# Plain fp32 products in place of the three-product high/low split, with ten slots for weight slabs

## The reference, cut to what matters

```python
def merge(h, fa, db, nc):
    gates = jax.nn.sigmoid(h @ w_g + b_gate)
    g_a, g_b, g_c = jnp.split(gates, N_BRANCH, axis=-1)
    return (g_a * (fa @ w_a) + g_b * (db @ w_b) + g_c * (nc @ w_c)) @ w_out

def conv_ffn(h, w_up, conv_w, conv_b, w_down):
    u = dwconv3(h @ w_up, conv_w, conv_b)
    a, b = jnp.split(u, 2, axis=-1)
    return (jax.nn.silu(a) * b) @ w_down

def _swiglu(x, w_in, w_out):
    a, b = jnp.split(x @ w_in, 2, axis=-1)
    return (jax.nn.silu(a) * b) @ w_out
```

## Time and profile before

| what | value |
| --- | --- |
| median of 3 runs | 2890.88 us (2889.95 to 2892.99) |
| profiled execution, its own time | 2876.13 us |
| its span on the core | 2874.0 us |
| mean granted TensorE clock | 0.969 of full speed |
| TensorE matmuls (PE) | 2656.9 us busy, 92% of the span, 17744 records |
| TensorE weight loads (PEld) | 2317.1 us, 81% |
| VectorE (DVE) | 1699.3 us, 59%, 2800 instructions |
| ScalarE (ACT) | 1335.0 us, 46%, 2136 instructions |
| GpSimd (POOL) | 184.0 us, 6% |
| read from memory | 378.36 MB, 132 GB/s over the span |

### The profile page before, as it was taken

One profiled execution on the slowest core, in us unless ns is written; L12 is line 12 of the kernel. 1 busy time (PEld: TensorE's weight loads), 2 busy tenths in 40 slices (PEclk: granted clock), 3 DMA queues, 4 the chain that ended last, 5 costly groups with the idle time before them and its releaser, 6 DMA issues.

```text
span 2874.0 us, 42224 instructions
## 1 busy us (share of the span) xinstructions
PE 2656.9 (92%) x17744; PEld 2317.1 (81%) x17744; DVE 1699.3 (59%) x2800; ACT 1335.0 (46%) x2136; POOL 184.0 (6%) x239
## 2 busy tenths in 40 slices
PE   5997899998999999899998998999899999978999
PEld 3875676676777777778788997999799999975999
DVE  5245534435676666454556876666666675746665
ACT  5235533324444443454445554455544553565543
POOL 1000000000000000000000001110010110015110
PEclk8998999998999999899999999999999999988999
DMA  7223432122344444232344654644255455530464
GB/s 233 72 85 123 133 99 70 59 88 74 103 161 146 133 133 145 74 103 96 103 140 133 201 186 141 205 162 147 88 177 191 156 183 191 177 106 1 155 198 147
DMA packets 337388, 382.12 MB, mean 133 GB/s; under 512 B 7408, under 2 KB 301296, under 8 KB 337200
## 3 DMA queue, kind: packets, MB, share of 16 engines
q1 hardware_dynamic: 334656, 370.37, 39.5%
q0 software_dynamic: 2544, 9.06, 1.0%
HBM read 378.36 MB, written 1.05 MB: 132 GB/s over the span
## 4 chain that ended last, share of the span: by engine, by line
PE 75%; DVE 11%; ACT 10%; issue 2%; DMA 1%; POOL 0%; SPq 0%; ACTq 0%; DVEq 0%
PE PS L1182 20%; PE PS L1184 19%; PE PS L1183 19%; ACT WH L1521 3%; DVE WL L1842 3%; PE PS L1315 2%; PE PS L1199 1%; PE PS L1201 1%; PE PS L1200 1%; PE PS L1330 1%; DMA RAWB<-in_w_ada 1%; PE PS L1298 1%; DVE TMP L1909 1%; PE PS L1231 1%; PE PS L1213 1%
## 5 line engine op out<-in xcount | busy, mean ns | idle before, releaser
L1842 DVE TENSOR_TENSOR WL<-RAWB,WH 128x1024 fp32r<-128x1024 f32 (+1 forms) x709 | 848.7, 1207 | 608.2 <-ACT WH L1521 606.0
L1182 PE MATMUL PS<-AH,WH 128*128 128x256 f32 (+1 forms) x3072 | 972.8, 317 | 82.1 <-DVE AL L1914 31.0
L1183 PE MATMUL PS<-AL,WH 128*128 128x256 f32 (+1 forms) x3072 | 952.6, 310 | 0.0
L1184 PE MATMUL PS<-AH,WL 128*128 128x256 f32 (+1 forms) x3072 | 952.2, 310 | 0.0
L1521 ACT ACTIVATE WH<-RAWB 128x1024 fp32r<-128x1024 f32 (+1 forms) x709 | 721.9, 1034 | 255.6 <-PE PS L1184 215.6
L1182 PEld LDWEIGHTS PS<-AH,WH 128*128 128x128 f32 x3072 | 586.3, 191 | 157.5 <-issue 52.3
L1183 PEld LDWEIGHTS PS<-AL,WH 128*128 128x128 f32 x3072 | 587.1, 191 | 31.4 <-issue 0.8
L1184 PEld LDWEIGHTS PS<-AH,WL 128*128 128x128 f32 x3072 | 586.2, 191 | 31.7
L1182 PE MATMUL PS<-BH,WH 128*128 128x256 f32 (+1 forms) x1504 | 470.1, 313 | 8.1 <-DVE BL L2010 3.0
L1183 PE MATMUL PS<-BL,WH 128*128 128x256 f32 (+1 forms) x1504 | 457.9, 304 | 0.0
L1184 PE MATMUL PS<-BH,WL 128*128 128x256 f32 (+1 forms) x1504 | 457.8, 304 | 0.0
(11 more groups left out here) (309 smaller groups left out, 2629.7 us busy)
## 6 DMA issues: line engine op xcount, KB each, us to landing
RAWB<-in_f_in SPq DMA_DIRECT2D x88, 1024.0 KB, 5.1
RAWB<-in_w_in SPq DMA_DIRECT2D x52, 1024.0 KB, 5.1
RAWB<-in_w_ada SPq DMA_DIRECT2D x48, 1024.0 KB, 5.5
RAWB<-in_w_up SPq DMA_DIRECT2D x44, 1024.0 KB, 5.1
RAWB<-in_f_out SPq DMA_DIRECT2D x40, 1024.0 KB, 5.1
RAWB<-in_w_down SPq DMA_DIRECT2D x20, 1024.0 KB, 5.1
RAWB<-in_sb_qkv SPq DMA_DIRECT2D x12, 1024.0 KB, 5.1
RAWB<-in_w_out SPq DMA_DIRECT2D x8, 1024.0 KB, 5.2
```

The lines of the kernel that those rows point to most:

```text
L1182: pe.matmul(out, h, xh[:, 0:T], start=k == 0, stop=False)
L1183: pe.matmul(out, h, xl[:, 0:T], start=False, stop=False)
L1184: i = pe.matmul(out, l, xh[:, 0:T], start=False, stop=k == g.kt - 1)
L1842: dve.tensor_tensor(c.part("WL", p), c.raw(p.slab)[:, k0:k1, c0:c1], c.part("WH", p).bitcast(F32), ALU.subtract).then_inc(up("lo", ("lo", ...
```

## The change

All splitting is taken out. `AH` and `AL` become one fp32 buffer `A`, `BH` and `BL` become `B`; `WH`, `WL`, the pieces and the step `split` are gone, and TensorE reads its weights from the slab in `RAWB`. A tile of depth is one fp32 product. `NR` goes from 3 to 10. A slab's slot comes free when TensorE has used the slab (`used`). The results that were copied to a high part are now written straight to `A` or `B`: the shift after a norm, the product of the two halves in the feed-forward parts (by DVE), `sub_scale`, the outputs of the attentions and of the DFT. `w_out` of the first block reads `Y` directly, the factor 0.5 being put into the modulation (`ada_half`). The eight tiles for `kv_norm` are one DVE instruction each (`kv_mul`). The sigmoid of the gates in the last attention becomes exp, add 1 and reciprocal, and the step `sb_table`, which loads an activation table on ACT, moves from behind the gate's product to the first head norm of the queries.

```diff
-NR = 3
-NW = 4
+NR = 10
 SLAB = 2048
-PIECE = 1024
...
     for s in plan.slabs:
         if s.j >= NR:
-            old = plan.slabs[s.j - NR]
-            on.wait_ge(*(at("lo", old.first + len(old.cuts) - 1) if old.cuts else at("used_raw", old.j)))
+            on.wait_ge(*at("used", s.j - NR))
...
         elif kind == "mm":
...
-            on.wait_ge(*at("lo", s.p.p))
+            on.wait_ge(*at("raw", s.p.j))
             for k in range(g.kt):
-                xh, xl = c.operand(g.src, k)
-                h, l = hi[:, k, s.c:s.c + 128], lo[:, k, s.c:s.c + 128]
                 on.wait_ge(*at(*g.ready(k)))
-                pe.matmul(out, h, xh[:, 0:T], start=k == 0, stop=False)
-                pe.matmul(out, h, xl[:, 0:T], start=False, stop=False)
-                i = pe.matmul(out, l, xh[:, 0:T], start=False, stop=k == g.kt - 1)
+                i = pe.matmul(out, w[:, k, :], c.operand(g.src, k)[:, 0:T], start=k == 0, stop=k == g.kt - 1)
...
         elif kind == "mm_tok":
...
-                pe.matmul(out, h, wh, start=k == 0, stop=False)
-                pe.matmul(out, h, wl, start=False, stop=False)
-                i = pe.matmul(out, l, wh, start=False, stop=k == 7)
+                i = pe.matmul(out, c.m["A"][:, k, tk], c.raw(s.p)[:, k, :], start=k == 0, stop=k == 7)
...
         elif kind == "ada":
...
-            for k in range(4):
-                pe.matmul(out, sc_v[:, 4 * i + k, :], hi[:, k, :], start=i == 0 and k == 0, stop=False)
-                t = pe.matmul(out, sc_v[:, 4 * i + k, :], lo[:, k, :], start=False, stop=i == 1 and k == 3)
+            for k in range(8):
+                t = pe.matmul(out, sc_v[:, k, :], c.raw(s.p)[:, k, :], start=k == 0, stop=k == 7)
...
-        elif kind == "split":
...
-            act.activation(c.part("WH", p), c.raw(p.slab)[:, k0:k1, c0:c1], ACT.Copy).then_inc(up("hi", ("hi", p.p)), 1)
...
-        elif kind == "split":
...
-            dve.tensor_tensor(c.part("WL", p), c.raw(p.slab)[:, k0:k1, c0:c1], c.part("WH", p).bitcast(F32), ALU.subtract).then_inc(
-                up("lo", ("lo", p.p)), 1)
...
         elif kind == "nmul":
...
-            act.activation(AH[:, k, a0:a0 + W], x[:, 0:W], ACT.Copy).then_inc(up("acted", ("xhi", name, k)), 1)
+            for i, seg in enumerate(s.x):
+                cols = slice(i * 256, i * 256 + 256)
+                t = act.activation(A[:, k, cols], x[:, cols], ACT.Identity, bias=c.mod(seg[3][0], seg[3][1], k, seg[2]))
+            t.then_inc(up("acted", ("normed", name, k)), 1)
...
-            act.activation(BI[:, 768:864], c.bank(s.b)[:, 0:96], ACT.Sigmoid).then_inc(up("acted", ("ns_gate",)), 1)
+            act.activation(BI[:, 768:864], c.bank(s.b)[:, 0:96], ACT.Exp, scale=-1.0).then_inc(up("acted", ("ns_gate_exp",)), 1)
```

More of the change, by code:

```diff
@@ L135, with __init__ @@
 class Slab:
[L136 to L143, removed]
+    def __init__(self, j, w, k0, kt, c0, cols):
+        self.j, self.w, self.k0, self.kt, self.c0, self.cols = j, w, k0, kt, c0, cols
 class Plan:
-    def __init__(self, slabs):
-        self.known, self.slabs, self.steps, self.put_off = slabs, [], [], []
+    def __init__(self):
+        self.slabs, self.steps, self.put_off = [], [], []
         self.banks = Ring(self, 8)
@@ L213, in run_units, with slab @@
             yield
-    def slab(self, w, k0, kt, c0, cols, cuts=()):
-        j = len(self.slabs)
-        s = self.known[j] if self.known else Slab(j, w, k0, kt, c0, cols, list(cuts))
+    def slab(self, w, k0, kt, c0, cols):
+        s = Slab(len(self.slabs), w, k0, kt, c0, cols)
         self.slabs.append(s)
         return s
[L223 to L239, removed]
     def gemm(self, name, w, col0, ncols, T, src, ready, ev, kt=8, k0=0, width=256, fine=True, x=None, hook=None):
@@ L318, in ada @@
             for half in range(2):
[L319 to L323, removed]
+                s = self.slab(("w_ada", l), 0, 8, (c + 2 * half) * 128, 256)
+                self.add("ada", (l, c), n=half, b=b, p=s)
                 self.tick()
@@ L637, in kv_split @@
     def kv_split(self, k):
-        m = self.tmps.take()
-        x = ([("kv_norm",)], 256, 256)
-        self.add("nmul", ("kv_norm", "ffn1_norm1"), n=k, t=m, x=x)
-        self.add("nlow", ("kv_norm",), n=k, t=m, x=x[1:])
-        self.tmps.give(m, ("xlo", "kv_norm", k))
+        self.add("kv_mul", n=k)
     def swiglu(self, i, l, norm, nrm, mark):
-        ready = lambda k: ("xlo", norm, k)
+        ready = lambda k: ("normed", norm, k)
         self.mark(mark)
@@ L779, in gate_turn @@
             self.add("ns_gturn", b=b, t=g48)
-            self.banks.give(b, ("ns_gate",))
+            self.banks.give(b, ("ns_gate_exp",))
             self.sqs.give(g48, ("ns_gturn",))
@@ L880, in sum, with split @@
             plan.banks.give(self.b, ("sd", self.name))
-    def split(self, name, T, segs, W, a0=0):
+    def split(self, name, T, segs, W):
         plan = self.plan
@@ L908, in __init__ @@
     def __init__(self, plan, name, gain, first=None):
-        self.plan, self.name, self.gain, self.first, self.n, self.low = plan, name, gain, first, 0, None
+        self.plan, self.name, self.gain, self.first, self.n = plan, name, gain, first, 0
     def add(self, k, after):
```

317 lines of the change are left out of this document (90 added, 227 removed).

## The result

The kernel after takes 3271.58 us (median of 4 runs, 3268.26 to 3273.81) against 2890.41 us for the kernel before beside it (4 runs, 2882.74 to 2892.99). The ratio is 1.1323, with a 95% interval of 1.1299 to 1.1346: slower by 381 us, 88 us less slow than the forecast of 3360. The profiled execution took 3271.48 us, its span is 3269.7 us, and its mean clock is 0.993 (before 0.969).

The account below looks back on a forecast made before the run. TensorE, busy 2656.9 of 2874.0 us, was taken as the bound. The profiled 2876.1 + 599 for products - 129 given back = 3346, times 1.005 = 3363, taken as 3360; stated range 3270 to 3450, the forecast's own 3280 to 3440.

Parts of the forecast that it names:

- The products: On TensorE, one plain fp32 product per depth tile replaces the split products: +599 us, all on the path.
- What was given back: Time returned from TensorE's waits, other standing time, clock and restarts, summed to -129 us.
- `WL`: TensorE's waits for the weights' low parts, 44.1 us, would go, with 10 kept for slow first slabs: -34 us.
- Low parts after norms: TensorE's 66.0 us of waits for activations' low parts; the chain stays, its last copy and subtraction go: -27 us.
- The rest of the standing time: TensorE's remaining 107.0 us of many small waits, such as those in attentions; a third would return: -35 us.
- Clock and restarts: On TensorE, a fifth of the half-rate clock loss returns, -18 us; unhidden weight loads after waits, -15 us.
- The scale of 1.005: The sum on the profiled execution, 3346 us, was multiplied by 1.005 for the median of the runs: 3363 us.
- Costed at nothing: The load queue's new wait for TensorE's use of the slab ten back; ten slots give over 60 us of cover.
- Nothing given back: Rival, 8%: the fp32 tiles keep all the waits and each record costs 4 ns more, giving 3535 us.
- weight loads bare: Rival, 4%: stationary tiles load between records, 93 ns more on each of 10,640 records, near 4360 us.
- faster: Rival, 2%: plain products stream at the split products' rate, 0.231 us in place of 0.432, giving 2066 us.
- All of it is given back: Rival, 8%: as DVE and ACT halve, only the start of the standing time remains, giving 3221 us.

Follow-up runs that it names:

- the last experiment: The kernel after with the gate's sigmoid and the place of `sb_table` as they were before: 3283.35 us, ratio 1.1349.
- the thin experiments: Kernels whose weight split instructions touch one column only; both thinned in the kernel before: 2779.97 us, under plain products from `WH`: 3318.66 us.

## Why the prediction was right and where it was not

**The ladder.** One row is one run; standing time is span less busy TensorE of its profile.

```
run                                       median   step   TensorE stands   clock
before                                    2891.6              217.1        0.969
products plain, all splits there          3370.7  +479        147.3        0.983
 + weight split thin                      3318.7   -52        114.9        0.986
 + low parts of activations thin          3311.2    -7        107.3        0.988
 + high copies and their steps gone       3283.4   -28         92.0        0.992
   (the change with old tables)
 + tables moved: the kernel after         3271.6   -12         83.6        0.993
```

(The standing times are 2874.0 - 2656.9, 3365.7 - 3218.4, 3322.6 - 3207.7, 3308.8 - 3201.5, 3278.7 - 3186.7 and 3269.7 - 3186.1.) Priced products of 592 less all that was given back, 113 + 52 + 7 + 28 + 12 = 212, are the +380 between the medians.

**How near it came.** The median of 3271.58 lies 1.6 us above the lower end of the stated range, 3270 to 3450, and one of the four runs below it; it is outside the forecast's own range of 3280 to 3440. The direction, the price of a product and the kind of wait that is left were foreseen. That it lies just inside the range is luck: the four runs spread over 5.6 us, more than the distance to the edge. The errors in the products, in what was given back and in the scale all pointed the same way.

**The products: right.** Forecast +599, by the records of after +592. That two records of an fp32 product of this shape cost 0.432 us was read off the 32 records of `seq_dft`, and the weight slabs run at 0.2158 a record. The 512-column record, for which the trace of before had only a case with 64 rows, is 0.4294, the double less a little; the weight load stays hidden. The estimate of 437 ns for such a product, which the prediction worked out from the Trainium skill (TensorE: Matmul & The Clock Gate, Back-to-back issue gap), took the gap of 2.5 ns for each of four passes; the 0.4316 measured agrees with one gap a record, two a product. The four passes of true fp32 (the Trainium skill, FP8 and Floating Point Precision, TensorE Precision Notes) fit the measured 0.4316 us against 0.109 for one bf16 record: 3.96 to 1.

**What was given back: too small, and this is the step that failed.** Within the profiled executions the span grew by 395.7, so 592 - 395.7 = 196 us came back (189 with the mean step above), and the forecast was 129. Term by term:
- `WL`: 44.1 us before, 1.4 us for a slab now, so -43; forecast -34. Right in kind. The 10 us kept for slow first slabs were not needed: with ten slots TensorE waits 1.4 us for a slab, with three 2.7.
- Low parts after norms: 66.0 before, 21.8 now, so -44; forecast -27. The mechanism named, that the chain of the norm stays and its shift is late next, is what the waits show (line 1473).
- "The rest of the standing time" (107.0): now 83.6 - 1.4 - 21.8 = 60.4, so -47; forecast "a third", -35.
- Clock and restarts: forecast -18 and -15. The standing time fell by 133.5 in all, so 196 - 133.5 = 62 us came back inside the busy time. The trace of before has 31 stretches at half rate, 179.1 us, and TensorE was busy for 131.7 of them; that of after has 10, 48.8 us, 37.0 busy. If half of such busy time is lost, the clock cost 65.8 us before and 18.5 after: it gave back 47, where "a fifth" of 89, 18, was taken. (An estimate and an upper one: at half rate the records of 256 columns stood 0.214 us apart before, against 0.117, which is less than double.) It leaves 15 us for restarts, as forecast, though with the mean step only 8. The clock is the largest single term that was mis-sized.

The terms were mis-sized because the sum priced relief, that is, work taken off DVE and ACT. The ladder shows a second source: with all that work left in, the plain products alone gave 113 us back, 69.8 of them standing time and, by the same estimate, 24 of them clock (16 stretches at half rate, 113.2 us, 83.2 busy). A tile that holds TensorE for 0.432 us in place of 0.3465 covers a quarter more of every fixed chain beside it. The prediction has this as half a sentence ("the filler products between two links are longer") and no term for it. In this order relief comes after it, with 52 + 7 + 28 + 12 = 99 us. The two are not additive, and the shares hang on the order: weight split work is worth 115 us if it goes first, under short products, and 52 under long ones. What the runs show is that both are there, not that one is the greater.

**The scale of 1.005: wrong, worth 17 us.** The profiled execution of before stood 14.8 us under its median, that of after 0.1 us under. That offset is not a property to be carried as a factor. The 88 us are then 7 (products), 67 (given back, 196 - 129), 17 (scale) and -3 (rounding 3363 to 3360).

**Costed at nothing: right.** The load queue's new wait (2543.5 us in the queue, 1.4 us for TensorE) cost nothing. The prediction's "ten slots are over 60 us of cover" was a correct sum with nothing hanging on it: three do as well. That the tables fell under "a third" was too little: 12 us by themselves, as far as the last experiment can tell.

**The rivals.** Nothing given back (3535) and weight loads bare (4360) are out by the pitch and the waits; faster (2066) needed 0.179 us a record, and there is 0.2158. "All of it is given back", 3221, is 51 us below the result, the forecast 88 above: the time lay nearer that rival, which priced 270 us of return. The return itself, 196, lies about midway between 129 and 270; the scale made the difference. Against the rival stood the reciprocal and the multiplications after a norm, and the wait for the end of that chain is the longest left, 21.8 of the 83.6 us.

**The signs.** 10,640 weight-product records came (6944 + 2208 + 704 + 768 = 10,624, and 16 of the gate); TensorE 97% busy; DVE 783.3 for "near 750", ACT 554.0 for "near 500"; pitches 0.2158 and 0.4294.

**What stays open.** The 28 us for the high copies are a difference of two kernels that differ in several small steps at once (the copies of the feed-forward products, the steps ahead of `w_out`), and weren't taken apart. In the runs with thin weight splits nearly all weights are zero. Whether the values of the weights bear on the granted clock was not tested; the kernel after, with its true weights, has the highest clock of the ladder, 0.993.

## What to carry to other kernels

A kernel whose main engine becomes slower gives part of it back even when nothing else changes, since longer products cover more of the chains beside them: put a term for cover in the sum before the terms for relief, and don't price relief at its value under the old, shorter cover. Price the clock by how long the engine was busy in the stretches at half rate, which the trace has, and not by a guessed share. One wait's name is a poor price for the work behind it: 44.1 us named the weight split here, and the work was worth 115. And where products are split for accuracy, price the parts' type first: three bf16 records are 0.327 us a tile, three fp32r 0.34 to 0.354, one true fp32 product 0.432, and weigh the bits that the bf16 parts lose.

## What the runs showed of the hardware

- fp32r does not run at bf16's pace in this kernel: 0.1133 to 0.118 us a record of 256 columns and 0.229 of 512, against 0.109 and 0.216 with the same three products and the same program. Its weight loads are longer as well. First a group of the kernel before, then one of the bf16 version with more slots; the number to read is the mean in ns ahead of the second bar, 191 against 99:

```profile
L1184 PEld LDWEIGHTS PS<-AH,WL 128*128 128x128 f32 x3072 | 586.2, 191 | 31.7
```

```profile
L1184 PEld LDWEIGHTS PS<-AH,WL 128*128 128x128 bf16 x3072 | 304.6, 99 | 122.2 <-issue 3.8
```

- The pace of fp32 records was the same whatever else ran: 0.216 us in layer 0 of before, and 0.2158 in the kernel after with half the work on DVE and ACT.
- An activation over one column still took 196 ns of ACT (the group above), so 709 of them left 133 us of the copy's work in the thin experiments, and the thin subtractions left 161 us of DVE's. The worths of 115 and 52 us are lower bounds to that extent.
- A table load of ACT is 1.283 us, and in the last attention, where each step of a head norm takes a logarithm (line 1639) and an exponential (line 1641), the old order paid it at both: 13 loads more in all, 12 us of the whole by medians, a size that is not settled.
